# FFN up projections with the tokens stationary, and the product turned by TensorE transposes

## What is computed

```python
def swiglu(h, w1, w3, w2):
    return (jax.nn.silu(h @ w1) * (h @ w3)) @ w2

for layer in range(DEPTH):
    ...
    shift, scale, gate = jnp.split(c_act @ ada_w[layer, 1] + ada_b[layer, 1], 3, axis=-1)
    hn = rmsnorm(x, norm_g[layer, 1]) * (1.0 + scale[:, None, :]) + shift[:, None, :]
    x = x + gate[:, None, :] * swiglu(hn, ffn_w1[layer], ffn_w3[layer], ffn_w2[layer])
```

## Time and profile before

| | |
|---|---|
| median of 3 runs | 2310.3 us (2310.27 to 2311.89) |
| the profiled execution | 2310.15 us |
| its span, first to last instruction | 2308.4 us |
| TensorE matmuls busy | 2285.0 us, 99% |
| TensorE weight loads busy | 1958.6 us, 85% |
| VectorE busy | 1758.4 us, 76% |
| ScalarE busy | 949.2 us, 41% |
| DMA | 620.36 MB, 269 GB/s on average |

### The profile page before, as it was taken

The page is one execution under the profiler, slowest core; times in us unless marked ns, Lnnn a source line. Parts: engine busy times, 40 slices in busy tenths (PEclk is TensorE's granted clock), DMA queues, the critical chain, the costliest instruction groups (busy, mean ns, idle before and its releaser), DMA issues.

```text
span 2308.4 us, 35295 instructions
## 1 busy us (share of the span) xinstructions
PE 2285.0 (99%) x12502; PEld 1958.6 (85%) x12502; DVE 1758.4 (76%) x2179; ACT 949.2 (41%) x1170; POOL 173.2 (8%) x181
## 2 busy tenths in 40 slices
PE   8999999999999999999999999999999999999998
PEld 5578888888888888888888888888888888888887
DVE  6758889888878888888987767788886666656665
ACT  2011444534434443344455554554443344433344
POOL 0000006100000000000500000350000000000012
PEclk9999999999999999999999999999999999999999
DMA  9999888677777777777876666676775555555554
GB/s 390 421 378 421 351 323 296 230 279 273 292 287 276 290 273 283 281 286 286 312 293 254 260 254 246 242 258 256 290 273 211 189 183 194 186 184 190 191 203 160
DMA packets 86924, 620.36 MB, mean 269 GB/s; under 512 B 10305, under 2 KB 10565, under 8 KB 11849
## 3 DMA queue, kind: packets, MB, share of 16 engines
q1 hardware_dynamic: 85682, 616.75, 70.2%
q10 hardware_dynamic: 1176, 2.74, 0.3%
HBM read 617.34 MB, written 2.11 MB: 268 GB/s over the span
## 4 chain that ended last, share of the span: by engine, by line
PE 93%; DMA 4%; DVE 2%; issue 0%; ACT 0%; SPq 0%; DVEq 0%; ACTq 0%
PE ps L1360 51%; PE ps L1358 13%; PE ps L1363 13%; PE ps L1305 7%; PE ps L1292 4%; DMA adaw<-ada_dram 3%; PE ps L1269 2%; DVE adaw L849 1%; PE ps L1252 1%; DMA raw<-wts_dram 1%; PE ps L1254 0%; PE ps L1496 0%; PE ps L1316 0%; PE ps L1506 0%; PE ps L1322 0%
## 5 line engine op out<-in xcount | busy, mean ns | idle before, releaser
L591 ACT ACTIVATE whigh<-raw 128x1024 fp32r<-128x1024 f32 (+1 forms) x692 | 720.9, 1043 | 1002.3 <-PE ps L1360 966.6
L840 DVE TENSOR_TENSOR wlow<-raw,whigh 128x1024 fp32r<-128x1024 f32 (+1 forms) x692 | 841.9, 1219 | 274.3 <-ACT whigh L591 261.7
L1360 PE MATMUL ps<-hn,whigh 128*128 128x512 f32 x3232 | 1018.4, 396 | 0.0
L1360 PE MATMUL ps<-mid,whigh 128*128 128x512 f32 x1856 | 585.0, 396 | 1.0 <-issue 0.7
L1360 PEld LDWEIGHTS ps<-hn,whigh 128*128 128x128 f32 x3232 | 493.2, 189 | 0.2
L1358 PE MATMUL ps<-hn,wlow 128*128 128x256 f32 x1616 | 449.7, 278 | 0.0
L1363 PE MATMUL ps<-hn,wlow 128*128 128x256 f32 x1616 | 448.1, 277 | 0.0
L849 DVE CUSTOM_DVE_ANT_0 adaw<-adaw,cact 128x2048 f32<-128x2048 f32 x152 | 353.8, 2329 | 25.3 <-DMA adaw<-ada_dram 25.3
L1358 PEld LDWEIGHTS ps<-hn,wlow 128*128 128x128 f32 x1616 | 303.3, 188 | 73.9
L1363 PEld LDWEIGHTS ps<-hn,wlow 128*128 128x128 f32 x1616 | 303.9, 188 | 69.3
L1360 PEld LDWEIGHTS ps<-mid,whigh 128*128 128x128 f32 x1856 | 283.4, 189 | 2.1 <-issue 1.2
(11 more groups left out here) (222 smaller groups left out, 1423.7 us busy)
## 6 DMA issues: line engine op xcount, KB each, us to landing
raw<-wts_dram SPq DMA_DIRECT2D x386, 1024.0 KB, 4.8
adaw<-ada_dram SPq DMA_DIRECT2D x152, 1024.0 KB, 6.7
adaw_more<-ada_dram SPq DMA_DIRECT2D x24, 1024.0 KB, 17.2
raw<-ada_dram SPq DMA_DIRECT2D x16, 1024.0 KB, 12.6
work<-wts_dram SPq DMA_DIRECT2D x6, 1024.0 KB, 14.7
x<-xT_dram SPq DMA_DIRECT2D x4, 512.0 KB, 5.5
out_dram<-x SPq DMA_DIRECT2D x3, 512.0 KB, 2.8
lru_space<-lru_w_dram ACTq DMA_DIRECT2D x1, 1024.0 KB, 10.9
```

The costliest lines, as they stand in the source:

```text
L591: act.activation(whigh[:, (2 * s + h) % 4, 0:width], raw[:, place, h * HALF:h * HALF + width], ACT.Copy)\
L840: dve.tensor_tensor(wlow[:, half, 0:width], raw[:, place_of(s, skips), h * HALF:h * HALF + width], whigh[:, half, 0:width].bitcast(F32), A ...
L1360: ins = pe.matmul(ps[:, bank(kind, s), :], whigh[:, half, w], src[:, kk, :, :], start=kk == 0, stop=kk == kts - 1, skip_group_check=True)
```

## The change

In each layer the first two up bodies (four hidden tiles) stay as they are. The other up bodies are taken in pairs: a `gates` body multiplies `hn` by 512 columns of w1 and a `values` body by the same 512 columns of w3, both by `tokens_body`, with the tokens stationary and the weights streaming. Gates go to the banks 0 and 1, values to 2 and 3. A pair makes a quad of four hidden tiles. There are 3, 4 and 3 pairs in the three groups of a layer.

At the end of the gates ScalarE applies silu from PSUM (two instructions of 512 columns) into `silu_gates`. At the end of the values VectorE multiplies it by the banks 2 and 3 (two instructions) into `hidden_tokens`, which has tokens on the partitions. TensorE turns it by 8 transposes of 128 x 128 in float32 into the banks 4 and 5, after the first half of the body that follows (`turn=True`: the next gates body, or the group's first down body); ScalarE copies the high plane to `mid` from there and VectorE subtracts for the low plane, two instructions each. The layout of the weights in memory is changed to match. In `values` bodies VectorE's `units_of` stands at the head of the stage, ahead of the splits, in place of its end. Lines that are not shown below: the shape of the loops over pairs, the definition of the two views of `work` and of the PSUM view `turned_tiles`, and the arguments that pass `turn` on.

```diff
 UP = [2 * n // CH for n in GROUPS]
+PLAIN = [2, 0, 0]
+PAIRS = [(u - p) // 2 for u, p in zip(UP, PLAIN)]
+QUAD = 4
...
+        def pairs(q, b, pair, units):
+
+            body(b, gates, q, 0, pair, units)
+            body(b + 1, values, q, 0, pair + 1, units)
+            with eng.Fori(1, PAIRS[q]) as i:
+                body(b + 2 * i, gates, q, i, i * 2 + pair, units, turn=True)
+                body(b + 2 * i + 1, values, q, i, i * 2 + (pair + 1), units)
```

ScalarE's part of a body:

```diff
+                    if turn and s == 0:
+                        tile, count = turned_quad(kind, q, i)
+                        for b in range(2):
+                            act.wait_ge(S["hidden_turned"], turned_before(kind, count) + 2 * b + 2)
+                            act.activation(mid[:, bass.ds(tile + 2 * b, 2), 0, :], turned_tiles(b), ACT.Copy).then_inc(S["hidden_high"], 2)
                     if ahead:
                         split(*chunk, 0)
+                    if kind[:5] == "gates" and s == 3:
+                        tile, count = quad(kind, q, i)
+                        act.wait_ge(S["halves_multiplied"], n * 8 + 8 + CREDIT)
+
+                        act.wait_ge(S["hidden_product"], count)
+                        for j in range(2):
+                            act.activation(silu_gates[:, j, :], ps[:, j, :], ACT.Silu).then_inc(S["silu_ready"], 2)
+                        act.wait_ge(S["silu_ready"], count + QUAD)
+                        act.sem_inc(S["chunks_evicted"], CH)
```

VectorE's part of a body:

```diff
+                    if kind[:6] == "values":
+                        units_of(pair, units, s)
+                    if turn and s == 0:
+                        tile, count = turned_quad(kind, q, i)
+                        for b in range(2):
+                            dve.wait_ge(S["hidden_high"], count + 2 * b + 2)
+                            m = mid[:, bass.ds(tile + 2 * b, 2), :, :]
+                            dve.tensor_tensor(m[:, :, 1, :], turned_tiles(b), m[:, :, 0, :].bitcast(F32), ALU.subtract)\
+                               .then_inc(S["hidden_ready"], 2)
                     if ahead:
                         split(*chunk, 0)
 
-                    dve.wait_ge(S["halves_multiplied"], n * 8 + 2 * s + 2 + CREDIT)
-                    if kind in STORED:
+                    if not is_pair(kind):
+                        dve.wait_ge(S["halves_multiplied"], n * 8 + 2 * s + 2 + CREDIT)
+                    if kind[:6] == "values" and s == 3:
+                        tile, count = quad(kind, q, i)
+                        dve.wait_ge(S["halves_multiplied"], n * 8 + 8 + CREDIT)
+                        dve.wait_ge(S["silu_ready"], count + QUAD)
+                        for j in range(2):
+                            dve.tensor_tensor(hidden_tokens[:, j, :], silu_gates[:, j, :], ps[:, 2 + j, :], ALU.mult)\
+                               .then_inc(S["hidden_product"], 2)
+                        dve.wait_ge(S["hidden_product"], count + QUAD)
+                        dve.sem_inc(S["chunks_evicted"], CH)
+                    elif is_pair(kind):
+                        pass
+                    elif kind in STORED:
...
-                    units_of(pair, units, s)
+                    if kind[:6] != "values":
+                        units_of(pair, units, s)
```

TensorE's part:

```diff
+            def turn_quad(kind, q, i):
+
+                tile, count = turned_quad(kind, q, i)
+                pe.wait_ge(S["hidden_product"], count + QUAD)
+                pe.wait_ge(S["hidden_ready"], count)
+                for f in range(QUAD):
+                    for j in range(2):
+                        ins = pe.transpose(turned_tiles(f // 2)[:, f % 2, j * P:j * P + P], hidden_tokens[:, j, f * P:f * P + P], ident_f)
+                    if f % 2:
+                        ins.then_inc(S["hidden_turned"], 2)
+
+            def tokens_body(n, kind, q, i, turn, inner):
+
+                first_bank = 0 if kind[:5] == "gates" else 2
...
                             for k in range(2):
                                 kk = 4 * s + 2 * h + k
                                 w = slice(k * 512, k * 512 + 512)
                                 for first, a, b in ((kk == 0, 0, whigh), (False, 0, wlow), (False, 1, whigh)):
-                                    ins = pe.matmul(ps[:, 2 + j, :], hn[:, kk, a, tok], b[:, half, w], start=first,
+                                    ins = pe.matmul(ps[:, first_bank + j, :], hn[:, kk, a, tok], b[:, half, w], start=first,
                                                     stop=kk == KT - 1 and a == 1, skip_group_check=True)
                         ins.then_inc(S["halves_multiplied"], 1)
+                        if turn and s == 0 and h == 0:
+                            turn_quad(kind, q, i)
```

More of the change, by code:

```diff
@@ L113, in ffn, with ups @@
     def ffn(first, layer):
-        up, down = f"up{layer}", f"down{layer}"
+        up, down, gates, values = f"up{layer}", f"down{layer}", f"gates{layer}", f"values{layer}"
+        def ups(q, b, pair, units):
+            body(b, up, q, 0, pair, units, True)
+            body(b + 1, up, q, 1, pair + 1, units)
+        def pairs(q, b, pair, units):
[4 more added lines that the diff above has]
+                body(b + 2 * i + 1, values, q, i, i * 2 + (pair + 1), units)
         def group(q, pair, units):
             b = q * (UP[0] + DOWN) + first
[L118 to L122, removed]
+            if q == 0:
+                ups(q, b, pair, units)
+            pairs(q, b + PLAIN[q], pair + PLAIN[q], units)
             units = 0 if layer else units
-            with eng.Fori(0, DOWN) as i:
-                body(b + UP[0] + i, down, q, i, i + (pair + UP[0]), units)
+            body(b + UP[q], down, q, 0, pair + UP[q], units, turn=True)
+            with eng.Fori(1, DOWN) as i:
+                body(b + UP[q] + i, down, q, i, i + (pair + UP[q]), units)
         b = first + 2 * (UP[0] + DOWN)
@@ L131, in ffn @@
             group(1, 0, 0)
-            bodies(b, UP[2], up, q=2)
-            bodies(b + UP[2], DOWN - 1, down + "short", q=2)
+            pairs(2, b, 0, 0)
+            body(b + UP[2], down + "short", 2, 0, 0, 0, turn=True)
+            bodies(b + UP[2] + 1, DOWN - 2, down + "short", q=2, i0=1)
             body(b + UP[2] + DOWN - 1, down + "short", 2, DOWN - 1, 0, -1, last=True)
@@ L137, in ffn @@
                 group(q, q * (UP[0] + DOWN) + 40, 2)
-            bodies(b, UP[2], up, 64, 2, q=2)
-            bodies(b + UP[2], 2, down + "short", 70, 2, q=2)
+            pairs(2, b, 64, 2)
+            body(b + UP[2], down + "short", 2, 0, 70, 2, turn=True)
+            body(b + UP[2] + 1, down + "short", 2, 1, 71, 2)
             body(b + UP[2] + 2, down + "short", 2, 2, 0, 0)
@@ L214, in second_width, with is_pair, quad, turned_quad @@
     return HALF
+def is_pair(kind):
+    return kind[:5] == "gates" or kind[:6] == "values"
+def quad(kind, q, i):
+    return i * QUAD + 2 * PLAIN[q], i * QUAD + (2 * PLAIN[q] + q * GROUPS[0] + int(kind.replace("short", "")[-1]) * FT)
+def turned_quad(kind, q, i):
+    return quad(kind, q, PAIRS[q] - 1 if kind[:4] == "down" else i - 1)
+def turned_before(kind, count):
+    return count - 2 * PLAIN[0] * (int(kind.replace("short", "")[-1]) + 1)
 def place_of(s, raw_start):
@@ L297, in bass_trunk @@
             hn_high_ready hn_ready final_ready
-            silu_ready hidden_product hidden_high hidden_ready
+            silu_ready hidden_product hidden_turned hidden_high hidden_ready
             lam_abs lam_exp lam_ready
@@ L317, in flat @@
             return ap.rearrange("p a t -> p (a t)")
+        silu_gates = flat(work[:, 0:4, :]).rearrange("p (j n) -> p j n", j=2)
+        hidden_tokens = flat(work[:, 4:8, :]).rearrange("p (j n) -> p j n", j=2)
         def work_tile(i):
@@ L372, in bass_trunk, with turned_tiles @@
         ident_f = ident_r[:, :].bitcast(F32)
+        def turned_tiles(b):
+            return ps[:, 4 + b, :].rearrange("p (f t) -> p f t", f=2)
         def masked_blocks(b):
@@ L452, in full_body, with body @@
                             load_unit(u + 2)
-            def body(n, kind, q, i, pair, units, fresh=False, inner={}, last=False):
+            def body(n, kind, q, i, pair, units, fresh=False, inner={}, last=False, turn=False):
                 if kind in FULL:
@@ L1275, in raw_pair @@
                     ins.then_inc(S["halves_multiplied"], 2)
-            def tokens_body(n, kind, inner):
+            def turn_quad(kind, q, i):
[9 more added lines that the diff above has]
+                first_bank = 0 if kind[:5] == "gates" else 2
                 for s in range(CH):
@@ L1282, in tokens_body @@
                         half = (2 * s + h) % 4
+                        if s == 0 and h == 0 and is_pair(kind):
+                            pe.wait_ge(S["chunks_evicted"], n * CH + (2 if kind[:5] == "gates" and not turn else 0))
                         for j in range(2):
                             tok = slice(j * P, j * P + P)
-                            if s == 0 and h == 0:
```

(25 more changed lines are left out.)

## The result

The changed kernel takes 2384.8 us against 2310.9 us: a ratio of 1.032, interval 1.0307 to 1.0333, 74 us more. I had forecast 2357, with a range up to 2378.

A forecast was written before the change was run, and what follows sets the result against it. TensorE was taken as the bound, busy 99% of the span. From 2310.15 us, -21.2 stream, +18.4 transposes, +45.5 stalls, +1.3 restarts and +3.3 new tiles made +47.3, so 2357 us; range 2338 to 2378.

The forecast's parts named there:

- The stream: TensorE's matmuls in the 40 converted bodies: fewer instructions at equal columns save 0.53 us a body, -21.2 us.
- The transposes: 160 added float32 transposes on TensorE, one instruction and 0.115 us each with nothing beside them: +18.4 us.
- 0.22 as two instructions: Rival on TensorE's transposes: each runs as two instructions, 0.22 us, giving 2374 us; chance 15%.
- 0.057 by columns: Transposes priced by columns alone, 0.057 us each, +9 us; together with no late unit 2301 us, chance 3%.
- The product's lateness: VectorE's moved units wait twice for ada loads, so TensorE awaits silu x value: 13 pauses of 3.5 us, +45.5.
- The new tiles: Down bodies wait for just-transposed tiles: 1.2 us twice in short groups, some 0.3 behind stalls in full ones, +3.3.
- The clock: Rival: TensorE's clock falls in the 13 pauses, 1.75 us more each, 2380 us, or 2448 if four times as long; 7%.
- the partial stall: Rival: faster landings or silus off ScalarE's path shrink TensorE's stall in part, 2334 to 2345 us; chance 4%.
- no quad without units paused: In the other 7 quads the product is ready 1.5 us after the values body, inside the 2.72 us cover: no cost.

The follow-up runs named there:

- e5_double_turns: The changed kernel with ada loads issued earlier (2307.5 us), each of the 160 transposes made twice: 2324.6 us, ratio 1.006 to before.
- e3_busy_pause: The changed kernel with 14 idle matmuls ahead of TensorE's wait for the product in the 13 quads with long pauses: 2361.6 us, ratio 1.0221.
- e4_old_moved: The kernel before, with VectorE's unit ahead of the splits in all up bodies but each layer's first: 2480.6 us, ratio 1.0737.
- e9_one_back: The changed kernel with only the unit of the values bodies' second stage put back behind its splits: 2323.0 us, ratio 1.006.
- e1_moved_back: The changed kernel with VectorE's units of the values bodies put back at the end of their stages: 2315.0 us, ratio 1.0019.

## Why the prediction was wrong

The mechanism, its place and its count were right; the time was outside the range because I cut the clock off. Point by point:

- **The stream.** Forecast -0.53 a body, -21.2. A quad without a late unit gained 0.16 net; the transposes' 0.79 and the slower start of the matmul behind them (0.31 to its successor where 0.227 is usual, 1992.74 to 1993.05) are 0.87, so two bodies gained 1.03, 0.52 each. Right.
- **The transposes.** Forecast 0.115 each, +18.4. Measured 0.109 at the upper clock, with the slower start 20 x 0.87 = +17.4. Right; 0.22 as two instructions and 0.057 by columns fall by e5_double_turns. Part 4 of the Trainium skill's page "TensorE: Matmul & The Clock Gate" has about 275 ns: the trace has that as a duration (273 ns in the median of the row below), while the starts are 0.109 apart, and by the starts goes the time. The Terms of the same page of the Trainium skill call the transpose mode four times faster for FP32; from start to start the runs have a factor of two, 0.109 against 0.22 for the float32 product of the earlier trace rows.

The transposes of the changed kernel, from the view of line L1364 (shortest, median and longest in ns):

```profile
L1364 PE MATMUL ps<-ident_r,work x160: 270/273/474, 521.8 to 2304.1; 128*128 128x128 f32 x160
```

- **The product's lateness.** Forecast 13 pauses of 3.5 from two waits of 2.3 and some 4 us. Measured 13 pauses, 48.7 us in all, 3.75 each (from the start of the last matmul, less 0.227; the view of waits has 46.6); in the one shown the unit's waits are 2.47 and 4.04. The loads landed in 6.8 and 6.9 where the earlier trace rows have 6.7; as each tenth counts twice, that is the difference. Right, 3 us too small.
- **The new tiles.** Forecast +3.3, measured 2.0 of waits: right in place, 1.3 too large. Not foreseen: small waits of layer 0's short down bodies, 0.7 and 0.4 before (L1360 in its view of waits), are down to 0.3 (L1461), 0.8 less.
- **The clock.** This is the step that failed. I gave "the clock falls in the pauses" 7% and let the range stop at 2378, ahead of its own price of 2380. It fell in 12 of 13 pauses and cost 26 us by e3_busy_pause; the rival's 1.75 a pause, 22.8 in all, was near that. My reason against it was that before shows the upper level in every slice. But before has no such pause in its stream, and the row can't show a short fall anyway: a slice is 58 us long, and the changed kernel, with its twelve falls, prints the same forty nines. I had the mechanism that makes the pauses, with 3.5 us each, and should have asked of it what the clock does then as part of the forecast and not as a rival. Part 1 of the Trainium skill's page "TensorE: Matmul & The Clock Gate" has idle time bring the clock down. I cited it, made it wait for pauses longer than my own 3.5 us without a reason, and gave it no weight. The trace of the changed kernel agrees with it (0.51 behind the pause above), and e4_old_moved has falls behind pauses of 2.2 us.

With measured sizes the sum is: -20.8 (40 x 0.52) + 17.4 + 48.7 + 0.7 (the first transpose behind a pause takes 0.05 longer to its successor, 13 times) + 2.0 - 0.8 + 26 = 73.2. The profiled execution is 73.1 us over the one before, 2383.27 against 2310.15. The 26 comes from e3_busy_pause, so the sum is a check. Without it the sum is 47.2, what I had forecast: the clock is the whole miss, and the small errors of the other terms cancel.

One slip in the working: the range is said to take in the partial stall, 2334 to 2345, but it starts at 2338.

Two things that I ruled out stayed ruled out: no quad without units paused, and nothing else became late behind VectorE's waits.

## What to carry to other kernels

When an operation is moved forward in an engine's order, look at when its data are sent for: a load that is issued behind a step of the same engine can't be early, and two of them in one deadline add up. Read the deadline on the engine that bounds the kernel, and if the reading gives it pauses of more than two microseconds, put the lower clock behind them into the sum (here 2 us a pause, 26 for 13) and into the range. A mean or a coarse row at the upper level doesn't say that the clock never fell; a window around the pause does. A gain that was masked can be had by issuing the load a stage earlier; here this turned 1.032 into 0.9987, and that is nearly all the form was worth.

## What the runs showed of the hardware

- A float32 transpose of 128x128 is one instruction, 0.109 us from start to start at the upper clock and 0.213 at the lower, where a float32 product of the same size is two instructions of 0.11.
- Pauses of 0.9 to 1.2 us (13 in e9_one_back) and of 1.0 to 1.4 us (15 in e4_old_moved) left the clock up. Of 30 of 2.2 to 2.6 us in e4_old_moved 15 brought it to 1.2 GHz, as did the one of 2.7 us in e1_moved_back. Of the 13 of 3.2 to 4.8 us in the changed kernel 12 did, and one of 3.9 us didn't. In the changed kernel the fall came in the second half of the pause or behind it, so it is mostly paid by the matmuls that follow. 14 matmuls in the pause prevented it in all 13, 7 in 7 of them. What decides in between stays open.
